# A gather issued one step earlier in the expert stage of a streaming encoder layer

## The reference, cut to what matters

```
s = sigmoid(t @ w_router);  sel = top_k(s + b_router, 8)      # 64 experts, 8 per token
out = silu(t @ w_s_gate) * (t @ w_s_up) @ w_s_down            # the shared expert
...
a, u = t @ w_e_gate[e], t @ w_e_up[e]                         # 1024 -> 128 each
out += (silu(a) * u * gate[token, e]) @ w_e_down[e]           # 128 -> 1024
```

## Time and profile before

| | us |
|---|---|
| median of 3 runs | 1190.78 (1189.35 to 1201.41) |
| profiled execution | 1198.63 |
| its span, first to last instruction | 1196.7 |
| TensorE matmul busy | 1070.6 (89%) |
| GpSimd busy | 358.0 (30%) |
| q1, SyncE's DMA queue | 181.20 MB, 41.0% of 16 engines' span |
| q0, GpSimd's DMA queue | 56.06 MB, 13.3% |

### The profile page before, as it was taken

The page is one execution under the profiler, slowest core; times in us unless marked ns, Lnnn a source line. Parts: engine busy times, 40 slices in busy tenths (PEclk is TensorE's granted clock), DMA queues, the critical chain, the costliest instruction groups (busy, mean ns, idle before and its releaser), DMA issues.

```text
span 1196.7 us, 24457 instructions
## 1 busy us (share of the span) xinstructions
PE 1070.6 (89%) x9716; PEld 644.8 (54%) x9716; DVE 498.0 (42%) x1249; ACT 367.6 (31%) x898; POOL 358.0 (30%) x411
## 2 busy tenths in 40 slices
PE   4899998899789966999999989999989899998596
PEld 2698895567764533455455545454545454554232
DVE  5437880264045577245416533332323232222146
ACT  4533432244244477311132222222222222222111
POOL 2233333323411243301023524343434343343100
PEclk9999998999899987899799989999989899999899
DMA  9322226654161000301375969797877879675596
GB/s 361 136 88 75 89 75 225 210 178 168 56 251 60 2 1 1 97 37 51 136 270 172 390 217 354 285 342 295 320 290 275 310 248 373 217 288 198 181 395 265
DMA packets 58417, 238.83 MB, mean 200 GB/s; under 512 B 22670, under 2 KB 22750, under 8 KB 46270
## 3 DMA queue, kind: packets, MB, share of 16 engines
q1 hardware_dynamic: 27792, 181.20, 41.0%
q0 software_dynamic: 30512, 56.06, 13.3%
HBM read 292.05 MB, written 47.40 MB: 284 GB/s over the span
## 4 chain that ended last, share of the span: by engine, by line
PE 74%; DMA 14%; ACT 4%; DVE 3%; issue 3%; POOL 2%; SPq 0%; DVEq 0%; POOLq 0%; ACTq 0%
PE bank L2061 16%; PE bank L2079 10%; DMA x_got<-x_dram,idx_tok 8%; PE bank L2043 5%; PE bank L1546 5%; PE bank L1548 4%; PE bank L1547 4%; PE bank L1869 4%; PE bank L2121 3%; PE bank L1574 3%; PE bank L1652 2%; PE bank L1963 2%; DMA w_stage<-in_w_in 1%; PE bank L1797 1%; DMA w_stage<-in_w_ada 1%
## 5 line engine op out<-in xcount | busy, mean ns | idle before, releaser
L2061 PE MATMUL bank<-slot,xt 128*32 128x256 f32 x4608 | 263.7, 381 | 6.9 <-issue 4.2
L2061 PEld LDWEIGHTS bank<-slot,xt 128*32 128x32 f32 x4608 | 151.3, 111 | 137.2 <-issue 50.3
L2079 PE MATMUL bank<-slot,hid_t 128*32 128x512 f32 x1152 | 144.6, 621 | 0.7 <-ACT hid_t L1511 0.7
L1546 PE MATMUL bank<-h_hi,w_hi 128*128 128x288 f32 x464 | 140.6, 303 | 0.0
L1547 PE MATMUL bank<-h_lo,w_hi 128*128 128x288 f32 x464 | 137.8, 297 | 0.0
L1548 PE MATMUL bank<-h_hi,w_lo 128*128 128x288 f32 x464 | 137.5, 296 | 0.0
L1505 ACT ACTIVATE sg<-bank 128x128 f32<-128x128 f32 x72 | 20.0, 277 | 279.8 <-PE bank L2061 279.8
L777 POOL TENSOR_TENSOR w_lo<-w_stage,w_hi 128x1024 fp32r<-128x1024 f32 x28 | 67.1, 2395 | 104.9 <-ACT w_hi L1242 104.8
L2043 PE MATMUL bank<-ident,x_got 128*128 128x128 f32 x576 | 78.8, 282 | 20.9 <-DMA x_got<-x_dram,idx_tok 20.9
L2564 DVE TENSOR_TENSOR hid<-sg,bank 128x128 f32<-128x128 f32 x72 | 20.7, 287 | 183.3 <-ACT sg L1505 175.1
L1546 PEld LDWEIGHTS bank<-h_hi,w_hi 128*128 128x128 f32 x464 | 88.2, 190 | 11.8 <-issue 11.4
(11 more groups left out here) (397 smaller groups left out, 1508.4 us busy)
## 6 DMA issues: line engine op xcount, KB each, us to landing
slot<-in_w_moe SPq DMA_DIRECT2D x65, 1536.0 KB, 9.1
w_stage<-in_w_ada SPq DMA_DIRECT2D x32, 512.0 KB, 5.1
pairs<-pair_dram SPq DMA_DIRECT2D x16, 1024.0 KB, 10.1
w_stage<-in_w_in SPq DMA_DIRECT2D x29, 512.0 KB, 3.7
resid<-in_w_ada SPq DMA_DIRECT2D x2, 2048.0 KB, 13.3
w_out_sb<-in_w_out SPq DMA_DIRECT2D x1, 4096.0 KB, 14.1
o_t<-in_x_t SPq DMA_DIRECT2D x4, 576.0 KB, 5.7
feat<-in_w_ada SPq DMA_DIRECT2D x1, 2048.0 KB, 18.6
```

The costliest lines, as they stand in the source:

```text
L1546: mm(out, hi_w, hi_x, start=first, stop=False)
L2061: ins = mm(bank[2 + i % 2][r, 0:2 * P], xt[:, i % 2, k, r], slot_of(place_no)[:, 2 * P * k:2 * P * (k + 1)], start=(k == 0), stop=(k == KD ...
L2079: ins = mm(bank[4 + 2 * (i % 2) + c][r, :], hid_t[:, i % 2, r], slot_of(place_no)[:, 2 * D + 512 * c:2 * D + 512 * c + 512], start=True, s ...
```

## The change

GpSimd's loop issues, in iteration i, the gather of step i + 4 where it issued that of step i + 3. The first iteration issues two, so that none is left out. The four places of `x_got` stay, and so do the gather's waits, loads and scatters.

```
             for i in range(1, N_STEPS + 1):
-                if i + 3 < N_STEPS:
-                    gather(i + 3)
+
+                for n in ((4, 5) if i == 1 else (i + 4,)):
+                    if n < N_STEPS:
+                        gather(n)
                 for n in over_places:
                     if SLOT_FOR[n][2] is not None and last_step_of(SLOT_FOR[n][2]) == i - 1:
                         load_over(n)
```

## The result

The changed kernel takes 1201.28 us (median of 20 runs) against 1192.62 for the kernel before (20 runs): a ratio of 1.0075, 95% interval 1.0039 to 1.0110. It is slower by 8.7 us, within 1%, and 8.3 us above 1193, the upper end of the range. The profiled execution took 1206.34 us.

A forecast was written before the change was run, and what follows sets the result against it. TensorE was taken as the bound, with six waits on late gathers, one per block. Stall-by-stall gains of 11.4 us, taken as 11.1, turned 1190.78 us into 1179.7 in the runs, range 1166 to 1193.

The forecast's parts named there:

- What bounds the kernel: TensorE's expert stage: six waits on late gathers, 20.9 us together, from a DMA backlog once per block of nine steps.
- The six gather waits go: TensorE's transposes: a gather's lead grows from 12.7 to 19.1 us, so all six waits, 20.9 us, vanish.
- No cost in GpSimd's waits: GpSimd's loop: the gather's later wait for transposes is already over, real only for gather 5; cost 0.
- The stalls turn into waits for the second load at steps 11, 38 and 47: Gate-and-up there waits for the overflow-only step's second overflow load: 5.8, 4.9 and 4.6 us; gains 1.3, 0 and 0.8.
- An overflow load keeps its issue and its place in GpSimd's DMA queue: GpSimd's DMA queue: one gather still precedes each load, so the load gains nothing from the move; step 11's lands at 695.0.
- three tenths of a us: Taken off the summed gain, 11.4 to 11.1 us, for rounding and gathers with more real rows ahead of the loads.
- The lower clock: Gate-and-up after the load waits at steps 11, 38 and 47 runs slower, 1.7 us each; bounds 5.1 more gain, 5.8 less.
- The sum: Stall by stall over the expert loop, loss before less loss after: gains together 11.4 us, taken as 11.1.
- Slower: GpSimd's DMA queue never empties, so step 1's extra gather delays each late overflow load 2.0 to 3.4 us: 1200; chance 0.10.
- Nothing measurable: Expert loop: loads take the stalls over entirely and the clock falls in each; gain 3.5 us, 1187; chance 0.17.

The follow-up runs named there:

- the third execution: The changed kernel with nothing altered, profiled a third time: loop 503.3 us, the overflow-only steps' second overflow loads landing after 16.1 us in the mean.

## Why the prediction was wrong, point by point

**What bounds the kernel** was read rightly: six gather waits, once per block, in a backlog of the DMA queue. But one execution gave their size. It lost 33.1 us in those blocks, and its loop was 6.3 us above the mean of three. Of its 7.85 us above the median the prediction knew, and carried the gain over unchanged.

**The six gather waits go**: right. None is left, and the slowest gather now took 16.8 us, within its lead of 19.1 (line 1172 of the changed kernel, as the earlier trace rows).

```profile
DMA to landing us min/median/max: 3.2/9.3/16.8
```

**No cost in GpSimd's waits**: nothing in the profile speaks against it; the instructions stand in the expected order, and only one gather waited for transposes, 4.0 us: that of step 5, as the prediction had it.

**The stalls turn into waits for the second load at steps 11, 38 and 47**: right in place and nearly in size. Forecast 5.8, 4.9 and 4.6 us of waiting, measured 5.78, 3.87 and 5.48.

**The step that failed** is this one: "An overflow load keeps its issue and its place in GpSimd's DMA queue", with the words that "only that gather's step number changes", for which three tenths of a us were taken off. The place is kept, the landing isn't. The gather ahead used to be that of the overflow-only step itself, whose places are mostly empty; now it is that of the full step after it. (By the 4 KB records of the scatters, an overflow-only step has about 20 real rows of 128 at most, and the step after it 110 or more.) In the changed kernel the load lands 2.1 us later in the mean, with the load ahead of that gather it lands after 12.3, and with the gather's rows taken out after 14.1 in the mean, as before. That the gather ahead makes it late is shown by the swap; that it is by its rows is shown in part, since step 20 kept its wait without them. Both kernels look alike at step 11 (17.7 and 17.7 us), the one block where the prediction compared gather and load; at step 20 it is 13.1 against 18.3. There the forecast left a wait of 0.99, and 6.35 came; at steps 29 and 56, where it had none to speak of, 1.92 and 2.10 (in the third execution 5.89 and 0.81). Steps 11, 38 and 47, where the forecast came out, are those where the load lands 1.0 us later at most, in the mean.

The Trainium skill, DMA: Bandwidth & Descriptors, section Queues, rings and completion order, was cited for the ring order. That order holds in every landing of GpSimd's queue that these profiles give. It says what stands ahead, and not how long it takes; the prediction let the count of transfers stand for their time.

**The lower clock** was a mis-sized term: 1.7 us at three steps, 5.1 together. The four gate-and-ups that ran slowly took 6.50, 5.05, 6.42 and 5.65 us instead of 3.64, 2.9 + 1.4 + 2.8 + 2.0 = 9.1 more. A mean of 2.3, inside the bounds that were kept, and one step more. The 1.7 came from one row, step 69, though the stalls that the prediction had before it cost more: beyond the idle time, the intervals of steps 11, 30, 38, 47 and 57 of the kernel before lost 2.3, 1.9, 2.5, 2.4 and 1.8 us, the idle times being 6.45 and 4.07 of the earlier trace rows and these:

```profile
822.93 1.20 PE L2043 MATMUL bank<-ident,x_got 128*128 128x128 f32 x8 [1.84 <-DMA x_got<-x_dram,idx_tok]
...
945.57 1.97 PE L2043 MATMUL bank<-ident,x_got 128*128 128x128 f32 x8 [4.70 <-DMA x_got<-x_dram,idx_tok]
...
1015.09 1.97 PE L2043 MATMUL bank<-ident,x_got 128*128 128x128 f32 x8 [2.75 <-DMA x_got<-x_dram,idx_tok]
```

So where the clock fell, a wait ahead of gate-and-up and one ahead of the transposes cost about the same. Nor did the row itself come again: in the changed kernel step 69 waited 3.27 us and its gate-and-up took 3.66, not 5.35.

```profile
1109.80 3.66 PE L2063 MATMUL bank<-slot,xt 128*32 128x256 f32 x64 [3.27 <-issue]
```

(The 2.80 us that the prediction set beside 4.88 run from the end of a gate-and-up, not from the transposes; from those it is 676.28 - 673.58 = 2.70.)

**The sum.** By intervals between gate-and-ups less 6.44, the profile after lost at step 11 and the one behind it (712.03 - 690.22 - 12.88) 8.9, where the forecast had 7.5; at steps 20 and 21 (784.71, the next start, less 757.44, less 3 x 6.44) 8.0, forecast 1.3; at step 29 2.1, forecast 0.2, what the kernel before loses there; at 38 and 39 6.8, forecast 6.6; at 47 and 48 7.7, forecast 6.3; at 56 2.3, forecast 0. Together 35.8 instead of 21.9. Half of the 13.9 us too much is step 20. With the 6.3 us by which the execution read was longer than the mean of three, they are about the 19.8 by which the forecast missed (11.1 gained, 8.7 lost).

**The rivals.** "Slower" came true in direction and in price per load (2.0 at its lower end, 2.1 measured) but not by its mechanism: GpSimd's queue does run empty. In the profile after, it moves no packet from 708.5 to 717 us, right behind the first block's stall, so no extra gather stays in front for good; the emptied gather doesn't bear on this, since less to carry would help either way. Its chance of 0.10 was too small. The second rival, "Nothing measurable", had the loads take the stalls over, as they did at steps 11, 38 and 47, but not the new ones at steps 20, 29 and 56. The profile had its warning: at steps 20 and 29 the load landed just as it was needed (757.6 and 817.1, each 0.1 before gate-and-up began), so any delay at all would show in full.

## What to carry to other kernels

Before a transfer is moved forward in a shared queue, ask for every transfer behind it not only how many stand ahead, but what they carry, and which of them has the least slack; the one with the least slack goes first. Here the change with that swap in seven iterations gives 0.9835, where the change alone gives 1.0075, and loads ahead of gathers without the change 1.0253.

One execution is a sample: in a loop whose stalls hang on a race of two DMA queues, three executions of the same kernel gave loops 11 us apart, as much as the effect in question.

## What the runs showed of the hardware that was not expected

Transfers that carry nothing aren't free. Reducing 39 empty indirect loads of 128 rows to one row each took 0.75% (0.40 to 1.10%) off the kernel before, and about 3% off the changed one (0.9762 against 1.0075), though the rows they skip move no weights. (The edit also makes them plain DMAs; the two aren't told apart.) The records of the kernel before show what an empty row may cost: from 686 to 692 us both queues were at work, and GpSimd's got through as many records as SyncE's, though its own carried 0.10 MB and SyncE's 2.43 (packets, MB, share of 16 engines):

```profile
q1 hardware_dynamic: 217, 2.43, 95.3%
q0 software_dynamic: 218, 0.10, 6.0%
```

The clock fell after a wait of 3.87 us (893.93: 6.42 us for gate-and-up) and not after one of 2.10 or 1.92 (3.66 us) in the profile after, but had fallen after one of 1.84 us at step 30 of the kernel before, where the step lost 3.7 us. At step 69 waits of 3.24 us before and 3.27 after cost 1.7 us and none; the granted clock was 0.84 from 1097 to 1108 us of the one and 1.00 from 1106 to 1118 of the other. The length of a wait alone doesn't tell what it costs.
